# Split keys before two attentions, queries in pieces, a norm that loads single rows, and a projection that ends with two row buffers

## The reference

```python
mod_l = jax.nn.silu(c) @ w_mod[l] + b_mod[l]
...
h_l = modulate(rmsnorm(x, norm1[l]), sh1, sc1)
...
return rmsnorm(x, final_norm)
```

```python
q = _rmsnorm(parts[0].reshape(b, s, N_HEADS, HEAD_DIM), q_gain)
k = _rmsnorm(parts[1].reshape(b, s, N_KV_HEADS, HEAD_DIM), k_gain)
...
o_att = jax.nn.silu(parts[3]) * _latent_attention(q, k, v, kc, vc)
...
out = jnp.concatenate([o_f, o_att, o_c, o_p], axis=-1) @ w_out
x_new = x + gate[:, None] * out
```

## Time and profile before

| | us |
|---|---|
| device time, median of 3 runs (lowest, highest) | 3560.42 (3559.0, 3563.74) |
| device time of the profiled execution | 3564.75 |
| its span, first to last instruction | 3563.0 |
| TensorE busy (share of the span) | 3214.0 (90%) |
| VectorE busy | 1852.6 (52%) |
| ScalarE busy | 1413.5 (40%) |
| GpSimd busy | 695.1 (20%) |
| TensorE's mean granted clock | 0.946 |

### The profile page before, as it was taken

One profiled execution on the slowest core, in us unless ns is written; L12 is line 12 of the kernel. 1 busy time (PEld: TensorE's weight loads), 2 busy tenths in 40 slices (PEclk: granted clock), 3 DMA queues, 4 the chain that ended last, 5 costly groups with the idle time before them and its releaser, 6 DMA issues. The chain is left out here.

```text
span 3563.0 us, 43053 instructions
## 1 busy us (share of the span) xinstructions
PE 3214.0 (90%) x17109; PEld 2595.1 (73%) x17109; DVE 1852.6 (52%) x2501; ACT 1413.5 (40%) x1941; POOL 695.1 (20%) x460
## 2 busy tenths in 40 slices
PE   7989998999999799793999999599988996998989
PEld 3867775778778677673878787488877775887867
DVE  4366785444444354646788888434416443152643
ACT  4222231433333244432777777431116434212640
POOL 2200001011111255200455555220001003000100
PEclk7999999999999899896999999799999997999999
DMA  6426555001000231324999999421112134211122
GB/s 200 117 80 209 182 170 184 31 24 44 24 26 24 59 116 58 131 103 184 359 378 388 379 389 372 143 66 52 38 34 54 48 113 154 61 43 44 48 72 83
DMA packets 247250, 470.72 MB, mean 132 GB/s; under 512 B 23936, under 2 KB 135673, under 8 KB 247053
## 3 DMA queue, kind: packets, MB, share of 16 engines
q1 hardware_dynamic: 231304, 410.09, 33.4%
q0 software_dynamic: 15264, 57.70, 4.9%
q10 hardware_dynamic: 484, 0.15, 0.0%
HBM read 405.34 MB, written 55.22 MB: 129 GB/s over the span
## 5 line engine op out<-in xcount | busy, mean ns | idle before, releaser
L2558 DVE TENSOR_TENSOR exp_wl<-wts_raw,exp_wh 128x2048 fp32r<-128x2048 f32 x144 | 394.3, 2773 | 105.9 <-ACT exp_wh L2518 105.9
L2518 ACT ACTIVATE exp_wh<-wts_raw 128x2048 fp32r<-128x2048 f32 x192 | 368.0, 1919 | 196.5 <-PE exp_gate L2447 64.1
L2724 PE MATMUL pr_ps<-l_h_high,pr_wh 128*128 128x512 f32 (+1 forms) x896 | 335.1, 374 | 0.0
L2725 PE MATMUL pr_ps<-l_h_low,pr_wh 128*128 128x512 f32 (+1 forms) x896 | 329.6, 368 | 0.0
L2726 PE MATMUL pr_ps<-l_h_high,pr_wl 128*128 128x512 f32 (+1 forms) x896 | 329.0, 367 | 0.0
L2417 POOL TENSOR_TENSOR exp_wl<-wts_raw,exp_wh 128x2048 fp32r<-128x2048 f32 x48 | 229.4, 4780 | 265.0 <-ACT exp_wh L2518 265.0
L842 PE MATMUL in_ps<-iw_h_high,in_wh 128*128 128x512 f32 (+1 forms) x696 | 268.7, 386 | 0.0
L843 PE MATMUL in_ps<-iw_h_low,in_wh 128*128 128x512 f32 (+1 forms) x696 | 263.8, 379 | 0.0
L844 PE MATMUL in_ps<-iw_h_high,in_wl 128*128 128x512 f32 (+1 forms) x696 | 263.3, 378 | 0.0
L2886 DVE TENSOR_TENSOR pr_wl<-pw_raw,pr_wh 128x512 fp32r<-128x512 f32 x84 | 57.7, 691 | 333.4 <-ACT pr_wh L2804 332.1
L1067 DVE SCALAR_TENSOR_TENSOR g_scratch<-g_scratch,g_c 128x512 f32<-128x512 f32 x240 | 181.8, 785 | 19.8 <-DVE g_scratch L1067 12.7
(11 more groups left out here) (515 smaller groups left out, 7222.8 us busy)
## 6 DMA issues: line engine op xcount, KB each, us to landing
wts_raw<-in_w_e_gate SPq DMA_DIRECT2D x64, 1024.0 KB, 9.6
wts_raw<-in_w_e_up SPq DMA_DIRECT2D x64, 1024.0 KB, 8.8
wts_raw<-in_w_e_down SPq DMA_DIRECT2D x64, 1024.0 KB, 7.6
g_scratch<-in_w_mod SPq DMA_DIRECT2D x80, 512.0 KB, 4.6
pw_raw<-in_w_in SPq DMA_DIRECT2D x88, 256.0 KB, 2.9
iw_raw<-in_w_in SPq DMA_DIRECT2D x74, 256.0 KB, 4.6
mod_w<-in_w_mod SPq DMA_DIRECT2D x4, 2048.0 KB, 11.7
wo_w<-in_w_out SPq DMA_DIRECT2D x2, 4096.0 KB, 13.6
```

The lines of the kernel that those rows point to most:

```text
L2518: act.activation(wh[:, m % RING], raw[:, m % RAW_RING], ACT.Copy).then_inc(high, 1)
L2558: dve.tensor_tensor(wl[:, m % RING], raw[:, m % RAW_RING], wh[:, m % RING].bitcast(F32), ALU.subtract).then_inc(low, 1)
L2724: nc.tensor.matmul(out, wh[:, slot, k, :], hi, start=h == 0 and k == 0, stop=False)
L2725: nc.tensor.matmul(out, wh[:, slot, k, :], lw, start=False, stop=False)
```

## The change

**Keys.** The split of the keys moves from `attention_2` into `project_in`: ScalarE rounds each key head twice (64x1280, one for each half of the partitions) after tiles 17 and 18, VectorE subtracts after tiles 19 and 20, and GpSimd clears the other half of `klo`. The split keys (`g.keys`) need memory that outlives the projection; they lie where the projection has its work buffers (`g.work`), which are dead by then.

**Queries.** They are split in pieces of two row tiles, straight from `g.parts` and without copies through DMA: three copies of 64x256 on ScalarE (`round_queries`) and two subtractions of 64x256 on VectorE (`rest_of_queries`). The first piece comes before the units, each later piece within the even unit ahead of the pair that uses it. GpSimd has nothing left to do in the attention, and SyncE only the prefetch for the Fourier branch.

**Norm.** In `FinalRows.sync` the context comes as two DMAs with a semaphore each, and `also` stands behind the eight rows; of it layer 0 keeps the table of sines, and the four weight halves are issued by ScalarE at the start of its block.

**First projection.** Two row buffers (`mrows`) with a semaphore each in place of one; five quarters in place of four in four early tiles (11, 12, 14 and 15), so that the last quarters belong to tile 35 and both last rows come inside the loop (at 36 and 37); the gates are copied at tile 34, turned at 35 and added at 36 in place of after the loop, in a place of their own (`kr`), which GpSimd clears.

```diff
     def sync(self, sp, also):
...
-        sp.dma_start(self.x[:, 0:CT, :], g.io["ctx_2"].rearrange("(t p) n -> p t n", p=P)).then_inc(self.ctx_in, 16)
+        for n in range(CT):
+            sp.dma_start(self.x[:, n, :], g.io["ctx_2"][n * P:(n + 1) * P, :]).then_inc(self.ctx_in[n], 16)
         sp.dma_start(self.fn, spread(g.io["final_norm"])).then_inc(self.fn_in, 16)
-        also(sp)
         sp.wait_ge(g.scattered, 16 * N_EXP)
         for n in range(LT):
             sp.dma_start(self.x[:, CT + n, :], g.x1[n * P:(n + 1) * P, :]).then_inc(self.x_in[n], 16)
+        also(sp)
...
-            done += 1 if name == "xm" else 4 if done < 26 or i >= len(FIRST) - 4 else 3
+            done += 1 if name == "xm" else 5 if done < 28 else 4 if done >= 70 else 3
...
-        bias, mrow = g.scratch[:, 8 * BANK:9 * BANK], g.scratch[:, 9 * BANK:10 * BANK]
+        bias = g.scratch[:, 8 * BANK:9 * BANK]
+        mrows = [g.scratch[:, n * BANK:(n + 1) * BANK] for n in (9, 2 * NT)]
...
-        grow = bias[0:96, :]
+        grow = kr[0:96, 0:BANK]
...
+        GATES_OUT = AT["xm", KD - 1] + 3
...
+                    if (name, t) == ("xm", 1):
+                        pool.wait_ge(key_split, 1)
+                        pool.memset(grow[:], 0.0).then_inc(zeroed, 1)
...
+                    if i == GATES_OUT + 1:
+                        pe.wait_ge(grow_ready, 3)
+                        for q in range(4):
+                            mm = pe.transpose(gacc[:, q * 96:(q + 1) * 96], grow[:, q * P:(q + 1) * P], g.ident[0:96, 0:96])
+                        mm.then_inc(gt_full, 1)
...
-                    if n:
-                        act.wait_ge(row_out, 32 * n)
+                    if n >= 2:
+                        act.wait_ge(row_out[n % 2], 32 * (n // 2))
+                    mrow = mrows[n % 2]
...
+                if not last:
+                    first_weights(act)
...
+                def round_key(j):
+                    act.wait_ge(rope_done, 3)
+                    act.wait_ge(d_done, 2)
+                    for side in range(2):
+                        act.activation(key_high[j][side * HD:(side + 1) * HD], g.parts[j * HD:(j + 1) * HD, K_AT, :],
+                                       ACT.Copy).then_inc(key_rounded, 1)
...
+                    if i in (17, 18):
+                        round_key(i - 17)
...
+                def key_rest(j):
+                    rows = slice(j * HD, (j + 1) * HD)
+                    dve.wait_ge(key_rounded, 2 * j + 2)
+                    step(dve.tensor_tensor(key_low[j][0:HD], g.parts[rows, K_AT, :], key_high[j][rows].bitcast(F32), ALU.subtract))
...
+                    if i in (19, 20):
+                        key_rest(i - 19)
...
+        def splits(u):
+
+            return u % 2 == 0 and u // 2 + 1 < n_pairs
...
+                    pe.wait_ge(q_done, 2 * (n // 4) + n % 2 + 1)
...
+                def round_queries(s):
+                    j, cols = two_tiles(s)
+                    src = g.parts[:, Q_AT + j, cols]
+                    act.activation(q[0:HD, 2 * j, cols], src[0:HD], ACT.Copy).then_inc(q_rounded, 1)
+                    act.activation(q[HD:, 2 * j + 1, cols], src[HD:], ACT.Copy).then_inc(q_rounded, 1)
+                    act.activation(q[0:HD, 2 * j + 1, cols], src[HD:], ACT.Copy).then_inc(q_rounded, 1)
+
+                round_queries(0)
...
                     if long[u]:
                         copy_four(u, "e0")
+                        if splits(u):
+                            round_queries(u // 2 + 1)
                         copy_four(u, "e1")
...
+                rest_of_queries(0)
                 maximum(0)
                 maximum(1)
...
                     if long[u]:
                         copy_odd(u)
+                    if splits(u):
+                        rest_of_queries(u // 2 + 1)
                     if u + 1 < len(units):
                         maximum(n + 3)
```

More of the change, by code:

```diff
@@ L2617, in half_tile, with key_parts @@
     sp.dma_start(g.raw[:, m % HALF_RING], view[m % 2][:, :, col:col + P]).then_inc(g.raw_in[m % HALF_RING], 16)
+def key_parts(g):
+    return [g.keys[:, j, 0:N_ALL] for j in range(KVH)], [g.keys[:, KVH + j, 0:N_ALL] for j in range(KVH)]
 def project_in(nc, g, l, last, streams, flat):
@@ L2680, in evicted, with first_weights @@
             eng.wait_ge(freed[STEP[tile] % 2], STEP[tile] // 2 + 1)
+        def first_weights(eng):
+            for m in range(HALF_RING):
+                half_tile(eng, g, l, m)
         with nc.Block() as block:
@@ L2685, in first_tiles @@
                 def first_tiles(sp):
-                    for m in range(HALF_RING):
-                        half_tile(sp, g, l, m)
+                    if last:
+                        first_weights(sp)
                     sp.dma_start(sin[:], io["t_sin"]).then_inc(cs_in, 16)
@@ L3066, in attention_2 @@
         items = [(2 * j + side, q0, keys) for j, q0, keys in units for side in range(2)]
-        per_group = len(items) // KVH
+        n_pairs = len(units) // 2
         long = [keys > 4 * P for _, _, keys in units]
@@ L3636, in layer @@
         flat = g.parts[:].rearrange("p t n -> p (t n)")
+        keys = ExitStack()
+        with ExitStack() as before_keys:
+            g.work = sb("work", [P, 4, N_ALL + KEY_PAD], before_keys, tag=f"l{l}", side="right")
+        g.keys = sb("keys", [P, 4, N_ALL + KEY_PAD], keys, dt=FR, tag=f"l{l}", side="right")
         g.rq = sb("rq", [P, NT, H2], outer, tag=f"l{l}")
@@ L3659, in layer @@
                 attention_2(nc, g, l, last, lambda sp: second_operands(sp, g, l, streams))
+                keys.close()
                 fourier(nc, g, l, streams)
```

142 lines of the change are left out of this document (53 added, 89 removed).

## The result

| | before | changed |
|---|---|---|
| device time, median of 6 runs (lowest, highest), us | 3559.93 (3557.85, 3563.74) | 3537.34 (3530.94, 3545.38) |
| profiled execution, us | 3564.75 | 3534.49 |
| its span, us | 3563.0 | 3532.9 |

The ratio is 0.9935, with a 95% interval of 0.9921 to 0.9949. The forecast was 3538.5, the range 3530 to 3548.

What follows compares the result with a forecast made beforehand. TensorE was busy throughout the projections, so time was to be had where stages begin and end: 12.3 + 9.3 - 3.4 + 2.0 + 1.7 = 21.9 us off the median 3560.42 gave 3538.5, range 3530 to 3548.

Steps and rivals of the forecast that it cites:

- start of at0: Start of the first later attention: without the copies within SBUF the second exponential comes 12.3 us sooner.
- start of at1: Start of the second later attention: the same shorter chain to the second exponential gains 9.3 us.
- pieces, second exponential to the Fourier stage: Query pieces inside both attentions' units: 3.4 us lost, three at 0.7 and thirteen at 0.1.
- start of the norm: Second block's norm: fewer bytes ahead of the first lat row on SyncE's queue gain 2.0 us.
- close of the first projection: End of the first projection: earlier last row and gates gain 1.7 us, the middle of 0.8 and 2.7.
- A: Attention units: half of ScalarE's and VectorE's added time per piece reaches TensorE, 15.5 us lost, 3550.6; chance 0.11.
- D: Attention units: all 1.94 us of each piece stands in series on TensorE's path, 31 us, 3566; chance 0.02.
- B: Attention starts: TensorE at half clock through first scores and the unit behind, some 4 us more each, 3546; chance 0.05.
- Keys: Key splitting in the projections: some 8 us of ScalarE and VectorE work in each, costed at nothing.
- rival C: Projections: key roundings delay TensorE by their whole 8 us in each, 3554.7; chance 0.04.

Runs made afterwards that it cites:

- e2: Kernel before with only the norm's change (context in two DMAs, table behind the rows, first weights issued by ScalarE): 3559.65 us, ratio 0.9995.
- e3: Kernel before with only the first projection's change (two row buffers, five quarters in early tiles, early gates): 3558.95 us, ratio 0.9990.
- e10: e4 with TensorE's third turn of the values behind the first two scores: 3533.49 us, ratio 0.9924 to the kernel before.
- e11: e10 with four multiplications that nobody reads behind the third turn of the values: 3533.44 us, ratio 0.9923 to the kernel before.
- e4: Changed kernel with all query pieces but an attention's first made on GpSimd: 3536.21 us, ratio 0.9921 to the kernel before.
- e5: Changed kernel with the keys split at the attention's start again, without copies through DMA: 3557.37 us, ratio 0.9982 to the kernel before.
- e6: Changed kernel with the first weights on SyncE again, between gain and rows: first lat row 12.67 us after the first issue, pr0's last product at 375.02.

## Why the prediction was right

The steps against what was measured, in us; the first three from the profiles of before and changed, the last two shown alone by e2 and e3:

| term | forecast (bounds) | measured |
|---|---|---|
| start of at0 | -12.3 (11.3 to 13.2) | -12.1 |
| start of at1 | -9.3 (8.3 to 10.2) | -9.1 |
| pieces, second exponential to the Fourier stage | +3.4 (1 to 5.2) | +4.1 and +0.5 |
| start of the norm | -2.0 (1.4 to 4.5) | -3.2 |
| close of the first projection | -1.7 (0.8 to 2.7) | -1.9 |
| sum | -21.9 | -21.7 |

**Starts.** The chain was right term by term: scores after 2.06 where 2.0 was added up, second exponential after 8.0 in the middle of 6.9 and 8.8. What the clock alone can move shows in e10, with an earlier start of the scores: 6.88 at 1.00 and 8.43 at 0.63. The Trainium skill's rule that the throttled clock is the default and activity releases it (TensorE: Matmul & The Clock Gate, Part 1) would have given 11.3 for the term. The traces agree in that the low clock lies in the idle start (0.57 in the earlier trace rows) and 1.00 behind it, but the changed kernel's first scores ran between the levels, at 4.09 us, and the term was 12.1.

**Pieces.** Settled units were forecast at 0.1 and took 0.07. Mis-sized were the pieces without a hole: 0.7 each was charged for the first units and the short one, at the middle of 0 and 1.1. At0's first unit took 1.6 more, and not all of it need be the piece's: without one, at a clock of 1.00, e11 has 6.80 where the old unit took 6.24. Around the short unit it was 2.1 (1.44 - 0.68 + 1.30), since the first unit of the second key head, which was counted as a settled one, waits there too. At1's first unit took only 0.5 more, and that is luck: in the profile of before the old one stood at 7.37, but in e2 and e3, which have the old attention too, at 6.23, with a start of 18.1 in place of 17.1. Against these two the start of at1 gains 10.1 and its pieces cost 1.6 and 1.8. Only the sum of both is firm: at1 is 8.6 shorter than in before, 8.5 and 8.3 than in e2 and e3. By before alone the pieces' 4.6 stay within the bounds; by e2 and e3 they come to 5.7 and 5.9, above 5.2. That bound is not worked out either: three at 1.1 and thirteen at 0.1 are 4.6. Rivals A and D are out: e4, without the pieces, gains 2.4 us in at0 and 0.6 in at1 from the second to the last exponential. Of B, the unit behind the first scores did not run at half clock in the changed kernel (1.00 from 2657 to 2662 us).

**Keys.** Nothing was charged, and in pr0 nothing was paid (e2 against the changed kernel); rival C is out. The prediction saw the gain in the copies through DMA that fall away. In e5 they are gone too, the second exponential comes 8.9 us sooner than before, and yet the attentions are as long as before, for splitting the keys there costs 9 us in each. So the early split is needed for the gain. What the copies alone cost is not isolated: e5 also puts the second key head's split, which GpSimd made before, on ScalarE and VectorE ahead of the first units.

**Norm.** The size was too low, 2.0 for 3.2, and its parts were wrong. The prediction charged the table 1.5 and the weights little, since they "want the same engines". E6 puts 2.4 of the 3.2 down to the weights' move to ScalarE's queue; the 0.8 between e6 (12.67) and before (13.42) are left for the table and the split context. Counting the bytes ahead was right for the row's own queue; what failed is the assumption that bytes in another queue hold the row up as much. The Trainium skill's rule (DMA: Bandwidth & Descriptors, Issuing engines are not separate DMA queues) was read as leaving the table's 1.5 alone. The trace agrees with the half of it that says that DMAs of several engines interleave (581 packets beside 579). With the other half, that a second issuer only saves issue time, the runs don't agree: the weights, out of the row's queue, let it land 2.4 us sooner, and e6's rows did not land by their issue.

**Close.** The middle of the two bounds was right in size, but it was a middle and no working. Which of the row and the store holds the stage was left open ahead: the row did before, the store does now. The gain came from the last row's wait for the one buffer; no run shows a part of it for the gates.

The 8.4 us by which the two profiled spans differ beyond these terms are in stages that the change does not touch; the same kernel's second profile took 1.6 of them back in f0 and 3.2 in the merge (179.04), and gave 2.8 more in the first attention (598.16). So they are the spread of executions; why the first attention and the merge spread is open.

## What to carry to other kernels

Work that a stage does at its start, before TensorE has anything to multiply, is worth its full length, and a stage before it in which TensorE never waits can take it for nothing: look for operands whose last input is ready half a stage earlier. When small work is put into a loop, the settled turns are cheap if an idle stretch of that engine lies there, but price the first and the odd turns one by one, and give the work to an idle engine where there is one. For a chain that begins with loads, count the bytes that stand ahead of the first load in its own queue, and give what is needed later to another engine's queue. At the end of a stage, look for a last transfer that waits for its buffer.

## What the runs showed of the hardware

The issue of the table, one DMA, held SyncE for some 2.8 us before the change (the weights' issues end at 2284.77, the rows' begin at 2287.63), and for 0.47 behind the rows. It is not the table that makes an issue long: in e6 it was the first row's, 4.09. The rows in e6 landed one behind the other, 1.27 to 1.29 us apart for 0.52 MB each, though their issues lay 0.47 to 4.13 us apart. Two queues with work moved as many packets each (581 and 579 in 6 us), and the one with the smaller packets got 0.29 MB beside 2.12. GpSimd's subtraction of 64x256 took 0.72 where VectorE's took 0.42, and settled units were within 0.02 us of those of before with it beside VectorE's maxima. And one stretch of one program ran at a granted clock of 1.00 in one execution and at 0.58 in another, 1.6 us apart.
